# Four places where a weight slab is split sooner, in a two-block model on one core

## The reference, cut to what matters

```python
def first_block(...):                      # two layers
    for l in range(2):
        hn = rms_norm(h, attn_norm[l])
        proj = hn @ w_in[l]                # three mixers share one projection
        y_a = rwkv7_mixer(...)             # 4 heads of 64, a scan over 512 tokens
        y_b = retention_mixer(...)         # 4 heads of 64
        y_c = mla_mixer(...)               # 8 heads; q and kv come from low-rank latents
        h = h + concat([y_a, y_b, y_c]) @ w_out[l]
        gu = rms_norm(h, ffn_norm[l]) @ w_gate_up[l]
        h = h + (silu(gu[..., :2816]) * gu[..., 2816:]) @ w_down[l]
    return rms_norm(h, final_norm)

def second_block(...):
    # even layer: six projections (xa, za, xb, gb, gc, zb), a depthwise convolution,
    # a gated linear recurrence forwards and backwards, a short convolution, w_out, norm
    # odd layer: gated linear attention (4 heads) forwards and backwards, head norm, w_out, norm
```

## Time and profile before

| | us |
|---|---|
| median of 3 runs | 2118.84 (2118.39 to 2123.34) |
| profiled execution | 2119.92 |
| its span | 2118.1 |
| TensorE matmuls busy | 2010.8 (95%) |
| VectorE busy | 1124.9 (53%) |
| ScalarE busy | 824.2 (39%) |
| GpSimd busy | 92.5 (4%) |

### The profile page before, as it was taken

One profiled execution on the slowest core, in us unless ns is written; L12 is line 12 of the kernel. 1 busy time (PEld: TensorE's weight loads), 2 busy tenths in 40 slices (PEclk: granted clock), 3 DMA queues, 4 the chain that ended last, 5 costly groups with the idle time before them and its releaser, 6 DMA issues.

```text
span 2118.1 us, 29241 instructions
## 1 busy us (share of the span) xinstructions
PE 2010.8 (95%) x12552; PEld 1616.5 (76%) x12552; DVE 1124.9 (53%) x1566; ACT 824.2 (39%) x1160; POOL 92.5 (4%) x61
## 2 busy tenths in 40 slices
PE   6998799999999999888899999999999999889997
PEld 4875487888888887647688888887778777679886
DVE  7456755543344545567554434447667673543373
ACT  4246533322222323664332222235464653324362
POOL 4010120000000000103000000000000000100000
PEclk9999999999999999989999999999999999999999
DMA  5310011222322322100032232223222222222111
GB/s 210 110 60 23 2 43 60 100 87 82 119 100 69 121 90 82 40 1 23 27 108 90 86 121 88 86 95 119 100 80 99 81 80 99 80 71 79 60 51 40
DMA packets 26192, 167.35 MB, mean 79 GB/s; under 512 B 2896, under 2 KB 3152, under 8 KB 10192
## 3 DMA queue, kind: packets, MB, share of 16 engines
q1 hardware_dynamic: 26064, 165.48, 22.4%
HBM read 163.38 MB, written 2.10 MB: 78 GB/s over the span
## 4 chain that ended last, share of the span: by engine, by line
PE 87%; DVE 9%; ACT 3%; issue 1%; DMA 0%; DVEq 0%; SPq 0%; ACTq 0%
PE bank L670 25%; PE bank L671 24%; PE bank L672 24%; PE bank L696 5%; PE bank L901 3%; DVE ring_low L1920 2%; ACT ring_high L1397 1%; PE bank L802 1%; DVE bank L2155 1%; PE bank L915 1%; DVE arena L2168 1%; PE bank L1268 1%; PE bank L1287 1%; DVE arena L2219 1%; PE bank L889 0%
## 5 line engine op out<-in xcount | busy, mean ns | idle before, releaser
L670 PE MATMUL bank<-arena_split,ring_high 128*128 128x512 f32 x2188 | 869.3, 397 | 48.6 <-DVE ring_low L1920 37.1
L671 PE MATMUL bank<-arena_split,ring_high 128*128 128x512 f32 x2188 | 857.7, 392 | 0.0
L672 PE MATMUL bank<-arena_split,ring_low 128*128 128x512 f32 x2188 | 857.2, 392 | 0.0
L670 PEld LDWEIGHTS bank<-arena_split,ring_high 128*128 128x128 f32 x2188 | 414.6, 190 | 149.2 <-DVE ring_low L1920 27.5
L671 PEld LDWEIGHTS bank<-arena_split,ring_high 128*128 128x128 f32 x2188 | 414.6, 189 | 89.1 <-issue 4.5
L672 PEld LDWEIGHTS bank<-arena_split,ring_low 128*128 128x128 f32 x2188 | 414.3, 189 | 87.2
L1920 DVE TENSOR_TENSOR ring_low<-ring,ring_high 128x2048 fp32r<-128x2048 f32 (+3 forms) x161 | 344.4, 2140 | 176.6 <-ACT ring_high L1397 176.0
L1397 ACT ACTIVATE ring_high<-ring 128x2048 fp32r<-128x2048 f32 (+3 forms) x161 | 284.6, 1769 | 382.6 <-PE bank L672 379.8
L1415 ACT ACTIVATE arena<-bank 128x512 f32<-128x512 f32 x72 | 43.1, 598 | 291.5 <-DVE bank L1901 291.5
L1901 DVE TENSOR_TENSOR bank<-bank,rstd 128x512 f32<-128x512 f32 x72 | 50.3, 698 | 121.5 <-PE bank L672 121.5
L1366 ACT ACTIVATE arena<-bank 128x512 f32<-128x512 f32 (+1 forms) x73 | 42.3, 594 | 137.5 <-PE bank L672 62.6
(11 more groups left out here) (343 smaller groups left out, 1829.2 us busy)
## 6 DMA issues: line engine op xcount, KB each, us to landing
ring<-slabs_in SPq DMA_DIRECT2D x122, 1024.0 KB, 4.8
ring<-slabs_in SPq DMA_DIRECT2D x32, 704.0 KB, 4.1
con<-con_in SPq DMA_DIRECT2D x1, 2208.0 KB, 12.0
h<-x_in SPq DMA_DIRECT2D x4, 512.0 KB, 9.1
out<-arena SPq DMA_DIRECT2D x8, 256.0 KB, 2.0
ring<-slabs_in SPq DMA_DIRECT2D x3, 512.0 KB, 3.4
ring<-slabs_in SPq DMA_DIRECT2D x2, 768.0 KB, 4.4
arena<-gates_in SPq DMA_DIRECT2D x1, 1536.0 KB, 9.8
```

The costliest lines, as they stand in the source:

```text
L670: pe.matmul(out, weight[0], right[0], start=start, stop=False)
L671: pe.matmul(out, weight[0], right[1], start=False, stop=False)
L672: return pe.matmul(out, weight[1], right[0], start=False, stop=stop)
```

## The change

Four edits move the moment at which a slab is split.

1. Last projection: a new semaphore `out_half_used` is raised after k = 3 of n = 0, and `slab_freed` gives it to `prepare` in the place of the group's end, for `odd_out0_0` alone. Both calls of `prepare("odd_out0_1")` move ahead of the loop over the banks.
2. Output projection: m = 2 and 3 take the first four mix tiles and m = 2 the fifth (27 matmuls), then m = 0 and 1 are finished (12), then m = 2 (9) and m = 3 (12). The splits follow: ScalarE prepares `out{l}_2` ahead of m = 0, VectorE ahead of the add of m = 1.
3. First recurrent tile: `prepare("even_xa_za1")` comes after the sigmoids on ScalarE, and after `gated_inputs(0)`, ahead of `gated(0)`, on VectorE.
4. GpSimd's copy also waits for the split of `kv_up`.

```diff
@@ TensorE, output projection
-                for m in range(2, DT // 2):
-                    for k in MIX_ORDER[:-2]:
-                        out_product(k, m)
-                for m in range(DT // 2):
-                    for k in MIX_ORDER[-2:]:
+                def out_finish(m, ks):
+                    for k in ks:
                         mm = out_product(k, m)
                     mm.then_inc(psum_ready, 1)
                     enter(("o", l, m), "dve")
                     slab_group[slab_index[f"out{l}_{m // 2}"]] = len(order) - 1
+                for k in MIX_ORDER[:4]:
+                    for m in (2, 3):
+                        out_product(k, m)
+                out_product(MIX_ORDER[4], 2)
+                for m in range(2):
+                    out_finish(m, MIX_ORDER[-2:])
+                out_finish(2, MIX_ORDER[5:])
+                out_finish(3, MIX_ORDER[4:])
@@ TensorE, last projection
-                        product(bk[:, :], token_mix(k, j), w[k], k == 0, False)
+                        mm = product(bk[:, :], token_mix(k, j), w[k], k == 0, False)
+                    if n == 0 and k == 3:
+                        mm.then_inc(out_half_used, 1)
+                        slab_freed["odd_out0_0"] = out_half_used, 1
@@ ScalarE, prepare
-                        act.wait_ge(psum_ready, slab_group[slab_index[split_slabs[n - SLOTS]]] + 1)
+                        old = split_slabs[n - SLOTS]
+                        act.wait_ge(*slab_freed.get(old, (psum_ready, slab_group[slab_index[old]] + 1)))
@@ ScalarE, output projection
-                        prepare(f"out{l}_{m // 2}")
+                        prepare(f"out{l}_{max(m // 2, 1)}")
@@ ScalarE, recurrence, after the four sigmoids
+                if m == 0:
+                    prepare("even_xa_za1")
@@ ScalarE, and in the same way VectorE, last projection
+            prepare("odd_out0_1")
             for n in range(2):
...
-                        if j == 0:
-                            prepare("odd_out0_1")
@@ VectorE, output projection
-                residual(lambda m: ("o", l, m), lambda m: f"out{l}_{m // 2}", ...)
+                residual(lambda m: ("o", l, m), lambda m: f"out{l}_{(m + 1) // 2 if m < 2 else m // 2}", ...)
@@ GpSimd
                 pool.wait_ge(psum_ready, finished(("rv", l, 1)))
+                pool.wait_ge(slab_split, split_index[f"kv_up{l}"] + 1)
```

More of the change, by code:

```diff
@@ L496, in two_blocks @@
         gla_o_used = sem("gla_o_used")
+        out_half_used = sem("out_half_used")
         stored = sem("stored")
@@ L518, in two_blocks @@
         FF_HIGH, FF_LOW = list(range(13, 24)), list(range(24, 30)) + [4, 5, 6, 7, 52]
-        slab_group = {}
+        slab_group, slab_freed = {}, {}
         book = {}
@@ L2340, in _ @@
                 dve.wait_ge(cnt.sem, cnt.value)
-                residual(lambda m: ("o", l, m), lambda m: f"out{l}_{m // 2}", lambda m: pr(f"ffn_norm{l}", m), FN_HIGH, FN_LOW)
+                residual(lambda m: ("o", l, m), lambda m: f"out{l}_{(m + 1) // 2 if m < 2 else m // 2}", lambda m: pr(f"ffn_norm{l}", m), FN_HIGH, FN_LOW)
                 prepare(f"gu{l}_0")
```

## The result

The changed kernel takes 2095.93 us, the median of 4 runs (2089.88 to 2099.65). The kernel before, run beside it, takes 2118.61 us (4 runs, 2113.44 to 2123.34). The ratio on record is 0.9882, with a 95% interval of 0.9858 to 0.9906: 1.18% faster, where 1.03% was forecast; the two medians alone are 1.07% apart. The profiled execution took 2093.52 us, its span 2091.7.

What follows compares the result with a forecast made beforehand. TensorE, busy 95% of the span, was taken as the bound. Terms 12.04 + 6.73 + 0.41 + 2.70 = 21.9 us off 2119.92 gave 2098.0; with the median 1.08 us under that execution, forecast 2097.0, range 2093 to 2103.

Steps and rivals of the forecast that it cites:

- Output projection: Term for the wait at the out*_2 slab in both layers: stall gone, gain 5.39 + 6.65 = 12.04 us.
- 0.2 us margin: Output projection: the out*_2 slab is ready at 342.1, TensorE wants it at 342.37, so no stall, with 0.2 us to spare.
- First recurrent tile: Term for the wait before even_gb_zb0: of a 6.98 us stall 0.25 us stays, gain 6.73 us.
- Last projection: Term for the wait at odd_out1: TensorE also waits for odd_out1_1, so of 9.32 us only 0.41 us is gained.
- GpSimd's copy: Term for the q_nope split: freed of the copy it takes 1.75 us; 0.25 of 1.60 us stays per layer, gain 2.70 us.
- A: Margins missed: three stalls keep 0.5 to 1.5 us each, 1.5 to 4.5 us return, 2098.5 to 2101.5; larger remainders, chance 0.10.
- B: Before attention, GpSimd's copy draws out VectorE's rope products instead of the split: 2 x 3.79 us return, 2104.6; chance 0.04.
- C: Last projection gains all of its 9.32 us, the double wait having been misread: 2088; chance 0.03.
- D: Output projection: later splits queue behind adds and squares, three boundaries stall about 6 us per layer: 36 us lost, 2133; chance 0.03.
- E: Gain given back later, VectorE or ScalarE being the true limit of these stages: about 2115 to 2119; chance 0.04.

Runs made afterwards that it cites:

- e0: The kernel before run once more with no edit, as a control: 2118.92 us, ratio 0.9997.
- e5: The changed kernel with the edit of the first recurrent tile undone: 2100.89 us, ratio 0.9916.
- e3: The changed kernel with TensorE waiting for the second half's slab only ahead of k = 4 in the last projection: 2083.29 us, ratio 0.9836.
- e4: The kernel before with one edit alone, TensorE waiting for the second half's slab only ahead of k = 4: 2108.85 us, ratio 0.9963.
- e8: The changed kernel with GpSimd copying the rotated key twice, the second time over the first: one run, 2096.8 us.
- e2: The changed kernel with the new order of the 60 output projection matmuls but the old place of the splits: 2096.97 us, ratio 0.9901.
- e1: The changed kernel with the old order of the 60 output projection matmuls but the new place of the splits: 2098.21 us, ratio 0.9911.

## Why the prediction was right

**What bounds the kernel.** Right: the gain is time in which TensorE stood still or ran at 1.2 GHz, and the busy times of VectorE and ScalarE did not move.

**Output projection.** Forecast 5.39 + 6.65; the stages are 5.37 and 6.66 us shorter. That these agree to 0.02 us shows that nothing of the stall was left, for the price had been read from the same execution that they are compared with; against e0, where fewer slow matmuls follow the same waits of 3.54 us, the stages are 5.22 and 5.40 us shorter. The 0.2 us margin, counted back over 21 steps, came out at 0.22. A count of matmuls times a measured step is this good because the matmuls between two waits have no other wait in them.

**First recurrent tile.** Forecast 6.73; 6.82 between the two profiled executions, 6.2 against e5. The difference between these two is how many slow matmuls follow the same wait of 4.59 us, 11 before and 8 in e5; e0 has 31.7 us for the stage that took 32.3 in the execution shown before. The remainder is 0.22, not 0.25.

**Last projection.** The mechanism was right: TensorE also waits for `odd_out1_1`, and e3 and e4 show it by taking that wait away. The term "gain 0.41 us" was mis-sized. The wait did shrink by 0.45 us (6.31 to 5.86), but 8 slow matmuls followed it instead of 14, which gave the other 1.25; together 1.70. The stall was priced with its tail when it was to vanish, and without it when it was only to shrink.

**GpSimd's copy.** Forecast 1.35 in each layer, measured 1.24 and 1.25. The free split was taken as 1.75 us and is 1.76, so that was right. Of the 1.60 us 0.36 remain, not 0.25.

**The sum.** 21.9 forecast, 23.0 measured at these places by the first execution of the kernel before, nearly all of the difference from the last projection, and 21.1 by e0. The medians are 22.7 us apart. The forecast of 2097.0 is 1.1 us above the median. The four runs behind that median spread over 9.8 us, so the terms bear the forecast out, while so close a hit of the time is partly luck.

**The rivals.** A did not come: nothing was left at `out*_2` and 0.22 us at `even_gb_zb0`, where it had 0.5 to 1.5 us each. B's collision happened (0.68 us of rope product became 2.71), and e8 shows both that it grows with GpSimd's work and how far it is covered (one copy more costs TensorE nothing in layer 0 and 0.17 us in layer 1); its price of 3.79 us was read from a row that was itself drawn out. The Trainium skill ("SBUF — State Buffer", section "Who interferes with whom") has GpSimd's instruction keep VectorE's out until its end; the rows of e8 and of the changed kernel agree, both products ending 0.55 us after GpSimd's instruction. C did not come with the diff; with TensorE's wait for the second half put off (e3) the stall went, and the kernel took 2083.29 us where C had 2088. D did not come: the path to the end of the `out*_3` split is 351.33 - 339.26 = 12.07 us (12.3 in the working), inside what was there. E is ruled out for the first tile by e5 and for the output projection by the unmoved stages behind it; behind `q_nope` the first score matmul keeps its distance (22.38 and 22.41 us), and past it the mixers' scatter hides anything of a few us.

**A delay that the working did not have.** In the last projection TensorE restarts 0.68 us after the split ends (2059.80 + 2.29 = 2062.09, restart at 2062.77), where 0.05 us lay between the two in the output projection of before (343.72 + 2.29 and 346.06). The trace of the changed kernel shows what stands in that time: the instructions that wait for a bank (L644) and in `split_slab` (L666), in the window from 2060 to 2063 us (ns each, least, median and most; us of the first and the last start):

```profile
L644 PEldq EVENT_SEMAPHORE  x4: 51/51/51, 2062.3 to 2062.7; - x4
L666 PEldq EVENT_SEMAPHORE  x2: 51/51/51, 2062.1 to 2062.2; - x2
```

These six follow one another from the split's end to the restart, some 0.11 us apart. The length of the wait is not the reason, for in the odd layer TensorE waits almost as long for the split of `odd_qk2`, which ends at 1846.19 us, and restarts 0.05 us later:

```profile
1846.24 0.80 PE L671 MATMUL bank<-arena_split,ring_high 128*128 128x512 f32 x1 [5.62 <-DVE ring_low L1933]
```

That fewer wait instructions would shorten the delay was not tried.

## What to carry to other kernels

Price a wait of TensorE with the slow matmuls behind it, also where the wait only shrinks; the first microseconds taken off a long wait were worth the most here, for with them the slow matmuls went too. Compare with more than one execution of the kernel before, since the slow matmuls behind one and the same wait vary (with them, the two waits of 3.54 us cost 5.2 or 5.4 us in layer 0 and 5.4 or 6.7 in layer 1). Where a list of weights is built ahead of a loop, the loop waits for the last of them: put each wait ahead of its first use. Before a GpSimd operation is moved, look at which VectorE operation it will then lie over and how much idle time stands behind that one.

## What the runs showed of the hardware

Waits of 1.16, 1.50 and 1.67 us left the granted clock at 1.00 in their windows (e4, e2, e1). At the edited places waits of 3.54 us and more were followed by 7 to 14 slow steps, most of them 0.43 us. Between these no run here had a wait at an edited place.

The length of a wait alone does not tell whether the clock falls. In the mixers of e1 a wait of 3.66 us left it at 1.00, and in the changed kernel it fell to 0.50 about one us after a wait of 1.86 us, in a stretch with many short waits:

```profile
955.00:975.00 20.00, 13.84 (x419) 12.31 (x419) 15.88 (x22) 7.14 (x14) 6.86 (x5) 1.00 0.01 3
959.65 1.56 PE L890 MATMUL bank<-arena 64*64 64x64 f32 x91 [3.66 <-DVE arena L2213]
...
880.72 0.33 PE L821 MATMUL bank<-con,arena 128*128 128x128 f32 x1 [1.86 <-DVE arena L2181]
881.80:885.00 3.20, 3.20 (x10) 2.15 (x11) 2.68 (x13) 2.28 (x10) 0.00 (x0) 0.50 0.00 0
```

The first two lines are of e1, the last two of the changed kernel.

The exclusion of VectorE and GpSimd goes both ways: GpSimd's subtraction, begun beside VectorE's running split, took 3.79 us instead of 2.40, and VectorE's rope product, begun beside GpSimd's subtraction, 2.71 us instead of 0.68.

Stages in which TensorE has no long wait (feed-forward, input projection, tiles 1 to 7) repeat within 0.07 us between executions, while the mixers, with many short waits, vary by 2 to 3 us per layer between two executions of the same program and by 5 to 6 us over all eleven, with the granted clock between 0.94 and 0.98 in the windows shown. A gain of a few us is better read from the stage than from the whole run.
